# Other places for the weight buffers and other column orders in the matmuls of a gated hybrid decoder block

## The reference

```
u    = rmsnorm(x, norm_w)
proj = u @ w_in                      # 4096 x 24576
a_q, a_f, a_i, a_g, c_b, c_c, c_h, c_g  (2048 columns each), g_a, g_b (4096 each)
y_a  = rmsnorm(HGRN2 recurrence of a_q, a_f, a_i) * silu(a_g)
y_b  = c_b * causal_conv3(c_c * c_h) * silu(c_g)
m    = sigmoid(g_a + b_a) * (y_a @ w_branch_a) + sigmoid(g_b + b_b) * (y_b @ w_branch_b)
out  = rmsnorm(x + m @ w_out, final_norm_w)
```

## Time and profile before

| | |
|---|---|
| median of 3 runs | 2975.61 us (2974.91 to 2975.81) |
| span of the profiled execution, first to last instruction | 2972.4 us |
| instructions | 46667 |
| TensorE busy | 99% of the span, 17061 matmuls |
| VectorE, ScalarE busy | 57%, 44% |
| moved by DMA | 552.28 MB, mean 186 GB/s |

### The profile page before, as it was taken

How to read it: one execution, slowest core, us unless ns; L and a number is a source line. 1 busy time by engine, 2 the same in 40 slices (tenths; PEclk the granted TensorE clock), 3 DMA queues, 4 the chain that set the end, 5 groups by cost and what they waited for, 6 DMA issues and landing times.

```text
span 2972.4 us, 46667 instructions
## 1 busy us (share of the span) xinstructions
PE 2954.2 (99%) x17061; PEld 2585.2 (87%) x17061; DVE 1700.5 (57%) x1973; ACT 1311.9 (44%) x1526; POOL 6.9 (0%) x23
## 2 busy tenths in 40 slices
PE   9999999999999999999999999999999999999998
PEld 7888888888888888888888888888888888888887
DVE  7666666666665555555555555555555555555555
ACT  6444444444444444444444444444444444444444
POOL 0000000000000000000000000000000000000000
PEclk9999999999999999999999999999999999999999
DMA  7555555555556555555566666666666666666665
GB/s 242 178 177 168 170 174 174 171 171 169 174 169 190 187 185 184 182 188 188 186 187 185 185 188 184 185 184 188 185 185 187 184 185 188 184 207 205 207 206 193
DMA packets 550941, 552.28 MB, mean 186 GB/s; under 512 B 17217, under 2 KB 547826, under 8 KB 550898
## 3 DMA queue, kind: packets, MB, share of 16 engines
q1 hardware_dynamic: 550898, 551.71, 59.9%
HBM read 547.45 MB, written 4.19 MB: 186 GB/s over the span
## 4 chain that ended last, share of the span: by engine, by line
PE 99%; DMA 0%; DVE 0%; ACT 0%; ACTq 0%; SPq 0%; issue 0%; DVEq 0%
PE PS L833 64%; PE PS L828 33%; PE SC L874 1%; DMA XS<-in_x 0%; PE SS L874 0%; PE OB L883 0%; PE OB L884 0%; PE SC L864 0%; PE OB L882 0%; PE SS L889 0%; PE PS L819 0%; PE SC L819 0%; PE OB L819 0%; DVE WS L481 0%; ACT U L327 0%; ACT H L453 0%
## 5 line engine op out<-in xcount | busy, mean ns | idle before, releaser
L833 PE MATMUL PS<-U,WS 128*128 128x512 f32 x5632 | 1982.3, 396 | 0.0
L481 DVE TENSOR_TENSOR WS<-RAW,WS 128x1024 fp32r<-128x1024 f32 x1024 | 1249.4, 1225 | 1177.2 <-ACT WS L309 1146.2
L309 ACT ACTIVATE WS<-RAW 128x1024 fp32r<-128x1024 f32 x1024 | 1084.0, 1060 | 1591.9 <-PE PS L833 1589.2
L828 PE MATMUL PS<-U,WS 128*128 128x256 f32 x5632 | 1574.7, 282 | 0.5 <-DVE WS L481 0.5
L833 PEld LDWEIGHTS PS<-U,WS 128*128 128x128 f32 x5632 | 1053.3, 188 | 245.0
L828 PEld LDWEIGHTS PS<-U,WS 128*128 128x128 f32 x5632 | 1061.8, 189 | 8.8 <-issue 0.8
L833 PE MATMUL PS<-WS,U 128*128 128x512 f32 x1536 | 533.5, 390 | 0.0
L828 PE MATMUL PS<-WS,U 128*128 128x256 f32 x1536 | 430.8, 283 | 0.0
L833 PE MATMUL PS<-Y,WS 128*128 128x512 f32 x1024 | 361.7, 397 | 0.0
L833 PEld LDWEIGHTS PS<-WS,U 128*128 128x128 f32 x1536 | 287.3, 188 | 58.3
L828 PEld LDWEIGHTS PS<-WS,U 128*128 128x128 f32 x1536 | 290.1, 189 | 2.6
(11 more groups left out here) (161 smaller groups left out, 631.9 us busy)
## 6 DMA issues: line engine op xcount, KB each, us to landing
RAW<-in_w_in SPq DMA_DIRECT2D x768, 512.0 KB, 3.7
RAW<-in_w_out SPq DMA_DIRECT2D x128, 512.0 KB, 3.8
RAW<-in_w_branch_a SPq DMA_DIRECT2D x64, 512.0 KB, 3.7
RAW<-in_w_branch_b SPq DMA_DIRECT2D x64, 512.0 KB, 3.8
XS<-in_x SPq DMA_DIRECT2D x8, 512.0 KB, 9.5
XR<-in_x SPq DMA_DIRECT2D x16, 256.0 KB, 4.0
out_dram<-H SPq DMA_DIRECT2D x8, 512.0 KB, 4.2
FW<-in_final_norm_w SPq DMA_DIRECT2D x16, 128.0 KB, 3.8
```

Source lines behind the costliest of these rows:

```text
L309: act.activation(WS[s][:, :, 0:GW], RAW[s][:, :, :], ACT.Copy).then_inc(hi_ready, 1)
L481: dve.tensor_tensor(WS[s][:, :, GW:2 * GW], RAW[s][:, :, :], WS[s][:, :, 0:GW], ALU.subtract).then_inc(lo_ready, 1)
L828: return pe.matmul(bank[:, T:2 * T], stat_lo, both[:, 0:T], start=False, stop=stop, skip_group_check=True)
L833: op = pe.matmul(bank, stat_hi, both, start=first, stop=last, skip_group_check=True)
```

## The change

The four `WS` buffers are placed by hand: the first on a multiple of 256 bytes, each next one 8192 + 64 bytes on. To make room, `NW` and `LT` become parts of `GB`. Each group gets an order in which its matmuls go through the moving columns, and through the PSUM columns likewise, so that every sum still lands in its place: forward, backward, paired (4 columns of the first half, 4 of the second, and so on, 16 bytes each), or paired and backward.

```diff
         RAW = [sb(f"RAW{i}", [P, KC, GW]) for i in range(RING)]
-        WS = [sb(f"WS{i}", [P, KC, 2 * GW], F32R) for i in range(RING)]
+        ring = (nc.sbuf_base + 255) // 256 * 256
+        slot = KC * 2 * GW * 4 + 64
+        ctx.enter_context(nc.sbuf_tensor("ring", [P, (ring + RING * slot - nc.sbuf_base + 3) // 4], F32))
+        WS = [at(f"WS{i}", [P, KC, 2 * GW], ring + i * slot, F32R) for i in range(RING)]
...
-        NW = sb("NW", [P, KT])
+        NW = GB[:, 64:64 + KT]
...
-        LT = sb("LT", [P, 48])
+        LT = GB[:, 0:48]
...
+            def forward(t):
+
+                return t
+
+            def backward(t):
+
+                return t[:, ::-1]
+
+            def paired(t):
+
+                return t.rearrange("p (h l e) -> p l h e", h=2, e=4)
+
+            def paired_back(t):
+
+                return paired(t)[:, ::-1, ::-1, ::-1]
+
-            def split_product(bank, stat_hi, stat_lo, both, first, last):
+            def split_product(bank, stat_hi, stat_lo, both, first, last, order):
 
                 def with_lo(stop):
-                    return pe.matmul(bank[:, T:2 * T], stat_lo, both[:, 0:T], start=False, stop=stop,
+                    return pe.matmul(order(bank[:, T:2 * T]), stat_lo, order(both[:, 0:T]), start=False, stop=stop,
                                      skip_group_check=True)
 
                 if not first:
                     with_lo(False)
-                op = pe.matmul(bank, stat_hi, both, start=first, stop=last, skip_group_check=True)
+                op = pe.matmul(order(bank), stat_hi, order(both), start=first, stop=last, skip_group_check=True)
                 return with_lo(False) if first else op
...
-            def branch(i, turn0, group0, modes, a=None, first=False):
+            def branch(i, turn0, group0, modes, a=None, first=False, orders=(forward, forward, backward, forward)):
...
-            branch(0, CONV_TURN, CONV_GROUP, (channels,) * 4, a=NP - 1)
+            conv = (backward, paired_back, forward, paired)
+            branch(0, CONV_TURN, CONV_GROUP, (channels,) * 4, a=NP - 1, orders=conv)
...
-                group(turn, 0, CD, channels, U, 0, 0, g)
-                group(turn, CD, CD, channels, U, 0, 1, g + 1)
+                group(turn, 0, CD, channels, U, 0, 0, g, order=backward)
+                group(turn, CD, CD, channels, U, 0, 1, g + 1, order=paired_back)
                 pe.wait_ge(y_ready, 2 * NP)
-                group(turn, 2 * CD, CB, channels, Y, 0, 0, g + 2)
-                group(turn, 2 * CD + CB, CB, channels, Y, KB, 1, g + 3)
+                group(turn, 2 * CD, CB, channels, Y, 0, 0, g + 2, order=backward)
+                group(turn, 2 * CD + CB, CB, channels, Y, KB, 1, g + 3, order=paired_back)
...
                     group(OUT_TURN + TURNS_OUT * i, n * CD, CD, positions, U, 0, n, OUT_GROUP + 2 * i + n,
-                          u_wait=(m_ready, 1) if first and n == 0 else None)
+                          u_wait=(m_ready, 1) if first and n == 0 else None, order=(backward, paired_back)[n])
...
-                        op = positions(1, c % RING, U, c * KC, KT, (0, 1) if c < CD - RING else (b,))
+                        op = positions(1, c % RING, U, c * KC, KT, paired_back, (0, 1) if c < CD - RING else (b,))
```

More of the change, by code:

```diff
@@ L832, in split_product, with channels @@
                     with_lo(False)
-                op = pe.matmul(bank, stat_hi, both, start=first, stop=last, skip_group_check=True)
+                op = pe.matmul(order(bank), stat_hi, order(both), start=first, stop=last, skip_group_check=True)
                 return with_lo(False) if first else op
-            def channels(par, s, rhs, k0, n_tiles):
+            def channels(par, s, rhs, k0, n_tiles, order):
                 for k in range(KC):
@@ L841, in channels, with positions @@
                                            WS[s][:, k, GW + t * P:GW + (t + 1) * P], rhs[:, k0 + k, :],
-                                           k0 + k == 0, k0 + k == n_tiles - 1)
+                                           k0 + k == 0, k0 + k == n_tiles - 1, order)
                 return op
-            def positions(par, s, lhs, k0, n_tiles, halves=(0, 1)):
+            def positions(par, s, lhs, k0, n_tiles, order, halves=(0, 1)):
                 for k in range(KC):
@@ L890, in attention, with group @@
                     op.then_inc(o_turned, 1)
-            def group(turn, n0, n_chunks, mode, operand, k_start, par, gidx, free=True, u_wait=None, a=None):
+            def group(turn, n0, n_chunks, mode, operand, k_start, par, gidx, free=True, u_wait=None, a=None, order=forward):
                 if free:
@@ L905, in group @@
                     op = mode(par, at_chunk % RING, operand[:, k_start:k_start + n_chunks * KC, :], c * KC,
-                              n_chunks * KC)
+                              n_chunks * KC, order)
                     op.then_inc(w_used, 1)
@@ L916, in group @@
                         pe.matmul(SC[0][:, 0:T], ONES[:, :], GA[:, 0:T], start=True, stop=True).then_inc(x_spread, 1)
-            def branch(i, turn0, group0, modes, a=None, first=False):
+            def branch(i, turn0, group0, modes, a=None, first=False, orders=(forward, forward, backward, forward)):
                 for n in range(4):
                     group(turn0 + TURNS_BRANCH * i, n * CD, CD, modes[n], U, 0, n % 2, group0 + 4 * i + n,
-                          free=not (first and n < 2), u_wait=(u_ready, KC) if first and n == 0 else None, a=a)
+                          free=not (first and n < 2), u_wait=(u_ready, KC) if first and n == 0 else None, a=a, order=orders[n])
             hgrn = (channels, channels, positions, channels)
@@ L926, in _ @@
                 branch(i, 0, 0, hgrn, a=i - 1)
-            branch(0, CONV_TURN, CONV_GROUP, (channels,) * 4, a=NP - 1)
+            conv = (backward, paired_back, forward, paired)
+            branch(0, CONV_TURN, CONV_GROUP, (channels,) * 4, a=NP - 1, orders=conv)
             with pe.Fori(1, NP) as i:
-                branch(i, CONV_TURN, CONV_GROUP, (channels,) * 4)
+                branch(i, CONV_TURN, CONV_GROUP, (channels,) * 4, orders=conv)
             with pe.Fori(0, NG) as i:
                 turn, g = MERGE_TURN + TURNS_MERGE * i, MERGE_GROUP + 4 * i
-                group(turn, 0, CD, channels, U, 0, 0, g)
-                group(turn, CD, CD, channels, U, 0, 1, g + 1)
+                group(turn, 0, CD, channels, U, 0, 0, g, order=backward)
+                group(turn, CD, CD, channels, U, 0, 1, g + 1, order=paired_back)
                 pe.wait_ge(y_ready, 2 * NP)
-                group(turn, 2 * CD, CB, channels, Y, 0, 0, g + 2)
-                group(turn, 2 * CD + CB, CB, channels, Y, KB, 1, g + 3)
+                group(turn, 2 * CD, CB, channels, Y, 0, 0, g + 2, order=backward)
+                group(turn, 2 * CD + CB, CB, channels, Y, KB, 1, g + 3, order=paired_back)
             def output(i, first=False, last=False):
```

## The result

The changed kernel takes **3067.07 us** (3066.68 to 3067.89), the kernel before 2975.71 in the same comparison: ratio 1.0306, 95% interval 1.0294 to 1.0318. It is 91 us slower; 2944 us were forecast, and the range ended at 3000.

What follows compares the result with a forecast made beforehand. TensorE's matmul spacing was taken to bound the kernel. A 2972.4 us span less 31 us for slow units, buffers at zero, gave 2941, and with 3.2 us from span to median 2944 us; range 2862 to 3000 us.

Steps and rivals of the forecast that it cites:

- The bound, the count, the method: Whole kernel: TensorE bounds it; time is the number of matmuls times their start-to-start spacing, read from windows.
- The price of a unit with a new order: 96 units of 64 pairs: 22.20 us for all 78 slow units (22.60 us before), no change for the rest.
- the nearest row: Price of new orders: the same two matmul instructions at their other observed rate, 22.20 us a group.
- The expected 31 us: Convolution and merge: gain from 78 slow units, 0.40 us each.
- 59% for faster: Whole kernel: chance of a gain over 0.2%, the forecast's 42% and rival B's 17% together.
- Rival E: Reversed or alternating reads run below a column per cycle; 8 paired units alone +155 us, 3131 us; 10%.
- The plain fp32 row: Level products, four matmuls of 192 columns in 0.65 us; the worst case, making a pair 650 ns.
- The buffers at zero: Weight buffers' new places: cost zero, as no instruction is added and write sizes stay.
- The slow rate: Convolution and merge: 22.60 us a group against 22.20, read as TensorE's weight load and moving stream meeting in step.
- Rival D: HGRN and output: the slow pattern spreads to the 50 units now fast; +20 us, 2996 us; 17%.
- Rival B: Changed units: new orders avoid half the constant 26.9 ns a pair; 83 us more gain, 2861 us; 17%.
- the 26.9 ns a pair: Every pair of matmuls: the fast rate's loss over 320 ns at full clock, 220 us over 8192 pairs.

Runs made afterwards that it cites:

- kick_kinds: The kernel before, all forward except the first one or two pairs (or the second) of convolution groups, in backward strips or backward; span 2951.5 us.
- every_fourth_all: The change with buffers 8192 bytes apart and every product reading every fourth block of 4 columns in four sweeps; 2842.49 us, ratio 0.9550 to the kernel before.

## Why the prediction was wrong

*The bound, the count, the method.* Right. TensorE's spacing is the time; the account above closes within it. Start and tail stayed, and VectorE and ScalarE stayed behind TensorE.

*The price of a unit with a new order.* This is the step that failed. My bounds were -2.12 and +19.4 us a unit, and I took "the nearest row", the other of the two forward rates: 22.20 us for every slow unit, nothing for the rest. That row is from another order; it said nothing of a read that jumps. Measured: strips +1.7 us on slow and +2.1 on fast units, 48 units, some 82 us; backward -0.01 in convolution and merge, +0.37 in the output. The expected 31 us didn't come either: the slow state did go, but what took its place was no faster. No row for 96 of 128 units was a reason to let the forecast stay near zero with both signs open; 59% for faster wasn't earned.

*Rival E.* Right in kind (the strips cost, in the paired groups alone), wrong in size by ten: 32 ns a pair on a fast unit, not 303. The plain fp32 row was no measure of it; why that row is slow, no run here shows. Its 8 paired units should have been 48, because paired backward costs the same. Its against, that each block of 16 bytes is used whole and has four columns' time, is true of the strips and didn't help: among blocks used whole, the distance decides.

*The buffers at zero.* Mis-sized: 7.1 us. All buffers were alike before, so the trace couldn't show it; I should have given this term its own bound.

*The slow rate.* That TensorE is in step with itself was right, and kick_kinds shows it as a state; the forward group behind strips ran at 22.20 us at the old places, as I had assumed. That any change of order gives the fast rate was wrong: three of four kicks in kick_kinds didn't, and backward groups at the old places stood at 22.48. Rival D's ground, that the kernel fell into the slow rate once, misread the trace: it enters and leaves it in each HGRN iteration from the second on.

*Rival B.* That the 26.9 ns a pair are no fixed price is borne out by every_fourth_all, where 13 of them went. B tied it to the wrong orders; that this loss is a meeting of weight load and moving stream is argued, not shown.

*The two pages of the Trainium skill.* The Trainium skill's page TensorE: Matmul & The Clock Gate (section "Step-by-step: what each phase is for") holds that the weight load takes nothing from the running matmul. Here, moving the weights alone by 96 bytes changed the channels groups from 22.20 or 22.60 to 22.475 us: the rate depends on where the weights lie, which by that rule it shouldn't, so the measurement stands against the rule for this fp32r stream. The Trainium skill's page Advanced Engine Details and Errata (section "Memory Cachelines") warns of non-contiguous PSUM patterns: writing in strips of 4 cost nothing here (22.55 us against 22.55 forward). It asks for two hits on a 16-byte line in SBUF; blocks of 2 columns have them and took 42.6 us, so two weren't enough here.

## What to carry to other kernels

When TensorE is busy throughout and its spacing is above columns over clock, the order and the place of its reads are worth a sweep: several orders fit into one kernel, one per group, and a window over each group reads them all in a single run. Here, 16-byte blocks taken 64 bytes apart gave 4.5% together with aligned buffers (2.7% with the buffers where they were, in one run), and blocks of 4 columns taken 128 to 1024 bytes apart lost 4 to 17% of a group against reading straight on. Before an effect without a row enters a forecast, it has both signs.

## What was unexpected of the hardware

- Reading moving columns straight on isn't the fastest: 22.20 to 22.60 us a group, against 21.37 in four sweeps at 64 bytes.
- Identical stretches of matmuls keep one of two rates, 22.20 or 22.60 us, for over a thousand us, by what ran before them.
- The rate depends on the weight buffers' place, and a move by 32 bytes counts; smaller moves weren't tried. The input never moved, so that the place counts relative to it is assumed.
- Past a group's first pairs, many rates are steps of about 3.33 ns a pair (333.3, 346.7, 353.3, 360.0, 366.7, 383.3 ns), eight columns' time. Why, and what memory layout makes 256 bytes the worst distance and 64 the best, stays open. That weight load and moving stream disturb each other is the reading that fits the moves of the weights; how they would do so is not shown.
